# Six raw slots that also hold the low parts, and four slots for the high parts of the split weights

## The chip, the core and the metric

The kernel runs on one core of a Trainium2 chip. A core has TensorE (PE in the profile; PEld is its weight load), VectorE (DVE), ScalarE (ACT), GpSimd (POOL) and SyncE (SP), which here issues nearly all transfers, and 16 DMA engines that bring weights from HBM to SBUF. The engines run programs of their own and wait for each other through semaphores. The metric is device time in microseconds for one execution; the figure given is the median of the runs.

## What is computed

Two blocks of a network for one sequence of 256 positions of width 1024, in float32. The part of the reference that matters here is the products with weights:

```python
def first_block(...):
    h = rms_norm(x, attn_norm_w[i])
    x = x + hybrid_mixer(h, ...)          # w_in (1024 x 7440), SSD and attention, w_ssd_out, w_attn_out, w_out
    h = rms_norm(x, moe_norm_w[i])
    x = x + hier_moe(h, ...)              # 32 experts: gate, up (1024 x 256 each), down (256 x 1024), top 2 of one group
    gate = jax.nn.sigmoid(rms_norm(x, ple_norm_w[i]) @ w_ple_gate[i])
    x = x + gate * (p[i] @ w_ple[i])
    return rms_norm(x, final_norm_w)
```

The second block takes that result: one wide input product, long convolutions by spectra (products with cosine and sine tables), latent attention with 8 heads (products w_uq and w_ukv), gates, and w_hy_out, w_attn_out and w_out.

## The kernel before

**Tiles of dense weights.** Every dense weight is cut into tiles of at most 2048 columns per partition, mostly four chunks of 128 rows by 512 columns (1 MB). There are 80 of them, numbered k in the order in which PE uses them; 42 stand before the experts and 38 behind. To keep float32 accuracy with fast products, each tile is split: SP loads it to a slot of `raw`, ACT copies it rounded to float32r into a slot of `WH` (line 1257), DVE subtracts, `WL = raw - WH` (line 1760), and PE makes three products per chunk, high by high, low by high, high by low (`mul3`, issued at line 519; transposes at line 528).

**Slots and waits.** `raw` has NRAW = 4 slots of 2048 columns, `WH` and `WL` have NSPLIT = 3 each: ten in all. ACT's copy of tile k waits for its load and for PE's use of tile k-3 (semaphore mark `("tile", k-3)`); DVE's subtraction waits for the copy; SP's load of tile k (`fetch`, line 2680) waits for the subtraction of tile k-4, `lo.wait_ge(e, k - NRAW)`.

**Where the splits stand.** ACT and DVE run in order. Calls of `weights(consumed)` stand between their other work; each makes the splits that `Splitting.due` allows, that is of tiles k whose forerunner in the slot is below `consumed`, so up to three ahead. `used(key)` is the number of tiles used when product `key` is done. Typical of ACT is: splits, then the drain of a product from PSUM, then splits. On ACT the drains and other steps are lines 1285 (`drain`), 1289 (`drain_t`), 1295 (sigmoid), 1416 (exponentials), 1671 and 1673 (drains of the key and value product `kv`). On DVE they are line 1800 (`drain_t`), 1867 (convolution), 2072 and 2089 (first block), 2396 (final norm of the first block), 2491 and 2492 (drain of `kv`), 2551 to 2567 and 2583, 2587 (products of the spectra and their results). Each PSUM bank is taken by a new product only when its last reader has drained it (`Ring.take`).

The stretch around `kv` on ACT and DVE is:

```python
            conv_T(1)
            for i in range(2):
                weights(used(("wuq", i)))
                drain_t((("kq", i), 1), KQ[:, 1, 384 * i:384 * i + 384])
            conv_T(2)
            for i in range(2):
                weights(used(("wukv", i)))
                mm.wait_ge(e, (("kv", i), 1))
```

**The experts.** 97 tiles of 1 MB (gate, up and down of 32 experts and `w_ple`) are loaded unsplit by `fetch_held` (line 2710) into 22 buffers. Twelve are parts of arrays that lie free by then, and ten are the slots of the dense tiles: the four raw slots and the six of `WH` and `WL`. The buffers have numbers; 9 to 12 were the raw ones, 13 to 18 the others. Which tile goes to which number is a fixed list, `buffer_of`, and a buffer is loaded again when PE has used its last tile (`held_last`). `held_raw` and `held_split` tell which numbers the dense slots have. Three early groups of expert loads (numbers 0 to 6) stand between the last dense fetches on SP. Behind the experts `weights(None, n)` makes the splits up to tile n at fixed places.

## Time and profile before

| what | value |
|---|---|
| time, median of 3 runs | 813.51 us (813.35 to 814.79) |
| profiled execution, its own time | 810.26 us |
| its span, from the first to the last instruction | 808.4 us |
| mean granted clock of TensorE | 0.973 |
| PE busy | 738.0 us |
| DVE busy | 466.5 us |
| ACT busy | 323.2 us |
| bytes read from HBM | 188.17 MB |

The profiled execution is one of its kind, and shorter than the median of the runs by 3.25 us. Busy time is the time in which an engine had an instruction running; PE's matmuls overlap, so that PE can be shown busy while it doesn't run at its full pace. In a group's row stand its count, busy time and mean of one in ns, then the engine's idle time in front of it and what ended most of that. The idle time in front of an instruction is put down to whatever released it last. The chain that ended last is followed back from the last instruction, step by step, to what released it, or to the instruction in front of it on the same engine.

### The profile page before, as it was taken

What the parts mean: (1) busy time and instruction counts of PE and PEld (TensorE: products, weight loads), DVE (VectorE), ACT (ScalarE), POOL (GpSimd) and SP (SyncE); (2) the same over time, 40 slices, a digit from 0 to 9 for tenths busy, and PEclk for the clock granted to TensorE, in tenths of its full rate; (3) what the DMA queues carried; (4) which work ended last, traced back from release to release, by engine and by line L of the source; (5) the groups of instructions that cost most, each with busy time, mean ns of one, the idle gap of its engine ahead of it and who ended that gap; (6) DMA issues with size and microseconds to landing.
All of it is one profiled execution on the core that took longest, in us unless ns stands there. A gap on an engine that the chain in (4) does not pass through costs nothing.

```text
span 808.4 us, 11003 instructions
## 1 busy us (share of the span) xinstructions
PE 738.0 (91%) x4608; PEld 557.3 (69%) x4608; DVE 466.5 (58%) x825; ACT 323.2 (40%) x479; POOL 17.8 (2%) x14
## 2 busy tenths in 40 slices
PE   4999999999999999996799797689999989799998
PEld 4978886878877886563445354247999856578886
DVE  5779965445866565531243131138677798855673
ACT  5554446536437334210110010036755524255631
POOL 0000000000000000000000000001100003000000
PEclk9999999999999999998789899999999999999999
DMA  9665543233438859799999999996462654333311
GB/s 318 186 213 195 188 141 125 81 105 104 124 112 326 326 223 424 316 372 419 420 420 419 421 422 422 418 388 222 134 233 89 229 186 153 108 105 105 104 53 53
DMA packets 62578, 189.98 MB, mean 235 GB/s; under 512 B 7417, under 2 KB 11771, under 8 KB 50044
## 3 DMA queue, kind: packets, MB, share of 16 engines
q1 hardware_dynamic: 60750, 184.44, 61.2%
q10 hardware_dynamic: 1774, 4.79, 1.7%
q8 instruction: 38, 0.62, 0.3%
q14 instruction: 16, 0.13, 0.1%
HBM read 188.17 MB, written 1.05 MB: 234 GB/s over the span
## 4 chain that ended last, share of the span: by engine, by line
PE 60%; DMA 16%; DVE 14%; ACT 8%; issue 2%; POOL 0%; SPq 0%; ACTq 0%; DVEq 0%
PE pb L519 56%; DMA raw<-in_w_exp_up 8%; DVE WL L1760 4%; PE pb L528 3%; ACT WH L1257 3%; DMA WHo<-in_w_exp_up 3%; DMA WLo<-in_w_exp_up 3%; DMA WLo<-in_w_exp_down 2%; ACT arena L1416 1%; DMA raw<-in_w_in 1%; DVE cv_ L1867 1%; DVE arena L2026 1%; ACT arena L1285 1%; POOL small L2658 0%; DVE arena L1813 0%
## 5 line engine op out<-in xcount | busy, mean ns | idle before, releaser
L1760 DVE TENSOR_TENSOR WL<-raw,WH 128x2048 fp32r<-128x2048 f32 (+5 forms) x80 | 173.4, 2178 | 87.3 <-ACT WH L1257 87.3
L1257 ACT ACTIVATE WH<-raw 128x2048 fp32r<-128x2048 f32 (+5 forms) x80 | 144.9, 1822 | 80.7 <-PE pb L519 71.2
L519 PE MATMUL pb<-WH,HTh 128*128 128x512 f32 (+2 forms) x384 | 156.1, 406 | 6.0 <-ACT arena L1285 3.1
L519 PE MATMUL pb<-WL,HTh 128*128 128x512 f32 (+2 forms) x384 | 148.5, 387 | 0.0
L519 PE MATMUL pb<-WH,HTl 128*128 128x512 f32 (+2 forms) x384 | 148.4, 386 | 0.0
L519 PEld LDWEIGHTS pb<-WH,HTh 128*128 128x128 f32 x384 | 72.8, 190 | 24.8 <-issue 5.1
L519 PEld LDWEIGHTS pb<-WL,HTh 128*128 128x128 f32 x384 | 72.7, 189 | 14.5
L519 PEld LDWEIGHTS pb<-WH,HTl 128*128 128x128 f32 x384 | 73.1, 190 | 13.2 <-issue 1.0
L519 PE MATMUL pb<-WH,arenao 128*128 128x512 f32 x192 | 59.6, 391 | 1.2 <-DVE arenao L1794 1.2
L519 PE MATMUL pb<-arena 128*32 128x256 f32 (+6 forms) x252 | 56.6, 422 | 3.4 <-ACT arena L1673 2.6
L2310 DVE TENSOR_TENSOR rt_<-rt_,pb 128x256 f32<-128x256 f32 x8 | 3.4, 421 | 90.2 <-ACT rt_ L1536 90.2
L519 PE MATMUL pb<-HTh,WH 128*128 128x256 f32 (+1 forms) x184 | 52.5, 285 | 0.2
L519 PE MATMUL pb<-HTh,WL 128*128 128x256 f32 (+1 forms) x184 | 52.0, 283 | 0.0
L519 PE MATMUL pb<-HTl,WH 128*128 128x256 f32 (+1 forms) x184 | 51.9, 282 | 0.0
L519 PE MATMUL pb<-arena,rt_ 128*32 128x512 f32 (+1 forms) x208 | 43.0, 462 | 0.7 <-DVE rt_ L2318 0.5
L1536 ACT ACTIVATE rt_<-pb 128x256 f32<-128x256 f32 x8 | 3.1, 383 | 100.0 <-PE pb L519 100.0
L519 PEld LDWEIGHTS pb<-arena 128*32 128x32 f32 (+4 forms) x252 | 27.1, 159 | 22.4 <-issue 8.8
L519 PEld LDWEIGHTS pb<-WH,arenao 128*128 128x128 f32 x192 | 35.7, 188 | 8.6 <-DVE WL L1760 1.4
L519 PE MATMUL pb<-WHo,arena 128*32 128x256 f32 (+1 forms) x96 | 30.7, 533 | 8.7 <-issue 4.4
L519 PE MATMUL pb<-WL,arenao 128*128 128x512 f32 x96 | 37.4, 390 | 0.0
L519 PEld LDWEIGHTS pb<-HTh,WH 128*128 128x128 f32 (+1 forms) x184 | 34.5, 188 | 0.9 <-DVE WL L1760 0.5
L519 PEld LDWEIGHTS pb<-HTh,WL 128*128 128x128 f32 (+1 forms) x184 | 34.6, 188 | 0.2
(366 smaller groups left out, 1267.7 us busy)
## 6 DMA issues: line engine op xcount, KB each, us to landing
raw<-in_w_in SPq DMA_DIRECT2D x46, 1024.0 KB, 5.2
raw<-in_w_exp_up SPq DMA_DIRECT2D x18, 1024.0 KB, 22.1
arena<-in_w_exp_down SPq DMA_DIRECT2D x14, 1024.0 KB, 13.1
arena<-in_w_exp_gate SPq DMA_DIRECT2D x13, 1024.0 KB, 21.0
raw<-in_w_out SPq DMA_DIRECT2D x8, 1024.0 KB, 5.2
WHo<-in_w_exp_down SPq DMA_DIRECT2D x8, 1024.0 KB, 19.0
WLo<-in_w_exp_down SPq DMA_DIRECT2D x8, 1024.0 KB, 22.2
raw<-in_w_exp_gate SPq DMA_DIRECT2D x7, 1024.0 KB, 13.8
```

The source lines that it names most:

```text
L519: return e.matmul(o, l, r, start=start, stop=stop, skip_group_check=True)
L528: return e.transpose(o, i, ident[0:k, 0:k])
L1257: e.activation(h_, r_, ACT.Copy).then_inc(hi.sem, hi.mark(k))
L1285: e.activation(dst[:, t, :], pb((name, t))[:, 0:n], f, scale=scale).then_inc(ac.sem, ac.mark((name, t)))
L1416: ins = e.activation(S1[s][:, cut], S1[s][:, cut], ACT.Exp, bias=nmx[:, s, t:t + 1], scale=-1.0, accum_out=ssum[:, t, h:h + 1])
L1536: e.activation(HG[q % 2], pb(("gu", q))[:, 0:256], ACT.Silu).then_inc(ac.sem, ac.mark(("su", q)))
L1760: e.tensor_tensor(l_, r_, h_.bitcast(F32), ALU.subtract).then_inc(lo.sem, lo.mark(k))
L1867: e.scalar_tensor_tensor(out=cv[:, s:L], in0=u[:, 0:L - s], scalar=cw[:, 3 - s, g:g + 1], in1=cv[:, s:L], op0=ALU.mult, op1=ALU.add).then_inc(
L2026: ins = e.scalar_tensor_tensor(out=LM[:, h, :], in0=pb(("lm", t, h0))[:, (h - h0) * 128:(h - h0) * 128 + 128], scalar=Ac[:, t, h:h + 1], i ...
L2310: e.tensor_tensor(HG[q % 2], HG[q % 2], pb(("gu", q))[:, 256:512], ALU.mult).then_inc(ve.sem, ve.mark(("gu", q)))
```

## The change

`WL` goes away. The low part is written over the raw weight, in the slot of `raw` (DVE reads `raw` and `WH` and writes `raw`, seen as float32r through `raw_r`). The ten slots are dealt out anew: NRAW = 6 and NSPLIT = 4. A raw slot is now free when PE has used the tile, not when the subtraction is made, so `fetch(k)` waits for `("tile", k - 6)`; ACT's copy waits for `("tile", k - 4)`. `due` gets a fixed distance, AHEAD = 3, which is what NSPLIT was, so that the splits stay at their places in the programs of ACT and DVE. The expert buffers 9 to 18 are named again in the order in which the slots come free: the raw slot of each of the last six dense tiles, and the high slot of each of the last four. All ten now wait for PE's use of a dense tile; the four raw ones had waited for a subtraction. SP's first loads are still issued as four, then two, though the two no longer wait for a slot; behind the experts six dense loads, not four, stand in front of two constants (lines 2762 and 2763).

```diff
--- before.py
+++ after.py
@@ -18,8 +18,9 @@
 L = 256
 D = 1024
 EPS = 1e-6
-NRAW = 4
-NSPLIT = 3
+NRAW = 6
+NSPLIT = 4
+AHEAD = 3
 SLOT = 2048
 SCRATCH = 1024
 CAP = 32
@@ -183,16 +184,15 @@
                    d_wr, d_late, d_filt, d_fw, d_hyb, d_bg, d_bg2, d_fb, d_out]
 
 
-        shared = (("WH", [128, NSPLIT, SLOT], F32R), ("WL", [128, NSPLIT, SLOT], F32R), ("HDh", [128, 1280], F32R),
+        shared = (("WH", [128, NSPLIT, SLOT], F32R), ("raw", [128, NRAW, SLOT], F32), ("HDh", [128, 1280], F32R),
                   ("HDl", [128, 1280], F32R), ("arena", [128, 18944], F32), ("cv_", [128, 1024], F32),
                   ("sg_", [128, 1024], F32), ("XN", [128, 2, D], F32), ("HTh", [128, 8, L], F32R), ("HTl", [128, 8, L], F32R))
         with ExitStack() as other:
-            WHf, WLf, HDhf, HDlf, arena_r, cv_r, sg_r, XN_r, *HTf = (
+            WHf, raw_r, HDhf, HDlf, arena_r, cv_r, sg_r, XN_r, *HTf = (
                 other.enter_context(nc.sbuf_tensor(n + "o", shape, F32 if dt is F32R else F32R))
                 for n, shape, dt in shared)
-        WH, WL, HDh, HDl, arena, cv_, sg_, XN, *HT = (sb(n, shape, dt) for n, shape, dt in shared)
+        WH, raw, HDh, HDl, arena, cv_, sg_, XN, *HT = (sb(n, shape, dt) for n, shape, dt in shared)
         HD_, HDf = (HDh, HDl), (HDhf, HDlf)
-        raw = sb("raw", [128, NRAW, SLOT])
         rt_ = sb("rt_", [128, 2048])
         PV = cv_[:, 512:1024]
         X = sb("X", [128, 2, D])
@@ -399,14 +399,15 @@
             for i in range(2):
                 weight((key, i), w, 8, 512 * i, 512, rows_)
         dense_again = len(tiles)
-        emptied = [(dense_again + i) % NSPLIT for i in range(NSPLIT)]
-        last_raw = [raws[(dense_again + i) % NRAW] for i in range(NRAW)]
+        emptied_raw = [(dense_again - NRAW + i, raws[(dense_again + i) % NRAW]) for i in range(NRAW)]
+        emptied_high = [(dense_again - NSPLIT + i, WHf[:, (dense_again + i) % NSPLIT, :]) for i in range(NSPLIT)]
+        emptied = [x for k in range(dense_again - NRAW, dense_again) for x in [*emptied_raw, *emptied_high] if x[0] == k]
         part = lambda o: arena[:, o:o + 2048]
         held = [part(16896), part(12800), rt_[:, :], part(4096), XN.rearrange("p t d -> p (t d)"), part(10752), part(6144),
-                part(14848), part(8704), *last_raw, *[x[:, s, :] for s in emptied for x in (WHf, WLf)], part(0), part(2048),
+                part(14848), part(8704), *[x for _, x in emptied], part(0), part(2048),
                 part(15168)]
         KF = [held[17], held[18]]
-        held_raw, held_split = (9, 10, 11, 12), 13
+        held_raw, held_high = (9, 10, 11, 13, 15, 17), (12, 14, 16, 18)
         FGU = [held[i].rearrange("p (c n) -> p c n", c=8) for i in (13, 14)]
         FD = held[15].rearrange("p (c n) -> p c n", c=2)
         held_to = {0: 0, 1: 0, 2: 0, 5: 0, 6: 0, 7: 0, 17: 44, 18: 44, 8: 56, 3: 68, 4: 76}
@@ -457,12 +458,13 @@
 
         def tile_parts(k):
             c, n = tiles[k]["shape"]
-            return tuple(x[:, tiles[k]["slot"], 0:c * n].rearrange("p (c n) -> p c n", c=c) for x in (WH, WL))
+            return tuple(x[:, 0:c * n].rearrange("p (c n) -> p c n", c=c)
+                         for x in (WH[:, tiles[k]["slot"], :], raw_r[:, k % NRAW, :]))
 
         def tile_flat(k):
             c, n = tiles[k]["shape"]
             s = tiles[k]["slot"]
-            return WH[:, s, 0:c * n], WL[:, s, 0:c * n], raws[k % NRAW][:, 0:c * n]
+            return WH[:, s, 0:c * n], raw_r[:, k % NRAW, 0:c * n], raws[k % NRAW][:, 0:c * n]
 
         def used(key):
             return chunk_at[key][-1][0] + 1
@@ -479,8 +481,8 @@
 
             def due(self, consumed):
                 while self.k < self.end:
-                    before = tiles[self.k]["before"]
-                    if before is not None and before >= consumed:
+                    first = 0 if self.k < dense_again else dense_again
+                    if self.k - AHEAD >= max(first, consumed):
                         return
                     self.k += 1
                     yield self.k - 1
@@ -1252,8 +1254,7 @@
                     if tiles[k]["before"] is not None:
                         mm.wait_ge(e, ("tile", tiles[k]["before"]))
                     elif k >= dense_again:
-                        i = held_split + 2 * emptied.index(tiles[k]["slot"])
-                        mm.wait_ge(e, held_last[i][0:2], held_last[i + 1][0:2])
+                        mm.wait_ge(e, held_last[held_high[k - dense_again]][0:2])
                     e.activation(h_, r_, ACT.Copy).then_inc(hi.sem, hi.mark(k))
 
             def norm_rows(n, src, after=None):
@@ -1577,7 +1578,7 @@
             weights(None, dense_again + 2)
             ss = norm_of["np"]
             e.activation(XN[:, 0, :], X[:, 0, :], ACT.Square, accum_out=ss[:, 0:1]).then_inc(ac.sem, ac.mark(("sq", "np")))
-            weights(dense_again)
+            weights(None, dense_again + 3)
             po.wait_ge(e, ("rs", "np"))
             weights(used(("wpg", 0)) - 1)
             junk = [rt_[:, 0:512], rt_[:, 512:1024]]
@@ -2369,7 +2370,7 @@
             low("np", NT, 8, pnw)
             weights(None, dense_again + 2)
             norm_sum("np", X)
-            weights(dense_again)
+            weights(None, dense_again + 3)
             weights(used(("wpg", 0)) - 1)
 
             def gated(i, t):
@@ -2672,7 +2673,7 @@
                 if dense_again <= k < dense_again + NRAW:
                     mm.wait_ge(e, held_last[held_raw[k - dense_again]][0:2])
                 elif k >= NRAW:
-                    lo.wait_ge(e, k - NRAW)
+                    mm.wait_ge(e, ("tile", k - NRAW))
                 c, n = tiles[k]["shape"]
                 dst = raws[k % NRAW][:, 0:c * n].rearrange("p (c n) -> p c n", c=c)
                 d = d_w[k % NRAW]
@@ -2700,10 +2701,8 @@
                     mm.wait_ge(e, ("mT", "T", 6))
                 elif i == 8:
                     ve.wait_ge(e, ("mg", 1))
-                elif i in held_raw:
-                    lo.wait_ge(e, dense_again - NRAW + held_raw.index(i))
-                elif i < held_split + 6:
-                    mm.wait_ge(e, ("tile", dense_again - NSPLIT + (i - held_split) // 2))
+                elif i < 19:
+                    mm.wait_ge(e, ("tile", emptied[i - 9][0]))
                 else:
                     mm.wait_ge(e, (("wo", 1), 1))
                 w = wpl if name[0] == "wpl" else dict(gate=wg, up=wu, down=wd)[name[0]][4 * name[1] + name[2]]
@@ -2713,7 +2712,7 @@
             xr = A["x"].rearrange("a (t p) d -> p (a t) d", p=128)
             for t in range(2):
                 e.dma_start(X[:, t, :], xr[:, t, :]).then_inc(d_x.sem, d_x.mark("in", by=16))
-            for k in range(NRAW):
+            for k in range(4):
                 fetch(k)
             for dst, src in ((rows[0:40, :], A["conv_w"].rearrange("a k (j p) -> (a k j) p", p=128)),
                              (rows[40:50, :], A["conv_b"].rearrange("a (j p) -> (a j) p", p=128)),
@@ -2730,7 +2729,7 @@
             turned_part = lambda a: a.rearrange("a n -> (a n)")[64:96].partition_broadcast(128)
             for dst, n in ((dtb, "dt_bias"), (alog, "a_log"), (dsk, "d_skip")):
                 e.dma_start(dst, bc(A[n])).then_inc(d_early.sem, d_early.mark("in", by=16))
-            for k in range(NRAW, 6):
+            for k in range(4, 6):
                 fetch(k)
             for dst, src in ((mnw, pc(A["moe_norm_w"], 8)), 
                              (snw, pc(A["ssd_norm_w"], 8)), (rb[:, 0:4], bc(A["b_router_group"])),
```

## Rows read from the trace of the kernel before

**Rows 1.** The page: busy shares, chain by engine, costliest groups with idle time before.

```profile
PE 738.0 (91%) x4608; PEld 557.3 (69%) x4608; DVE 466.5 (58%) x825; ACT 323.2 (40%) x479; POOL 17.8 (2%) x14
...
PE 60%; DMA 16%; DVE 14%; ACT 8%; issue 2%; POOL 0%; SPq 0%; ACTq 0%; DVEq 0%
...
L1760 DVE TENSOR_TENSOR WL<-raw,WH 128x2048 fp32r<-128x2048 f32 (+5 forms) x80 | 173.4, 2178 | 87.3 <-ACT WH L1257 87.3
L1257 ACT ACTIVATE WH<-raw 128x2048 fp32r<-128x2048 f32 (+5 forms) x80 | 144.9, 1822 | 80.7 <-PE pb L519 71.2
```

**Rows 2.** Who waited for whom, whole span: us in total, times, longest.

```profile
PE pb L528 <- DVE arena L2587: 4.3, 1, 4.3
...
PE pb L519 <- ACT arena L1285: 3.1, 4, 2.0
...
PE pb L519 <- ACT arena L1673: 2.6, 1, 2.6
...
PE pb L519 <- DVE WL L1760: 1.1, 1, 1.1
```

**Rows 3.** Busy time by stretch: PE, PEld, DVE, ACT, POOL, clock, DMA share, GB/s.

```profile
362.00:540.00 178.00, 146.30 (x1190) 72.32 (x1182) 43.16 (x101) 19.68 (x36) 0.00 (x0) 0.89 1.01 418
```

**Rows 4.** Timeline of DVE from 654 us: start, us, what, idle before.

```profile
654.37 0.67 DVE L2551 TENSOR_TENSOR XN<-pb,arena 128x512 f32<-128x512 f32 x1
...
655.38 0.69 DVE L2553 TENSOR_TENSOR sg_<-pb,arena 128x512 f32<-128x512 f32 x1 [0.33 <-PE pb L519]
656.10 0.69 DVE L2555 TENSOR_TENSOR XN<-XN,sg_ 128x512 f32<-128x512 f32 x1
```

**Rows 5.** Timeline of ACT from 255 us.

```profile
265.75 1.92 ACT L1257 ACTIVATE WH<-raw 128x2048 fp32r<-128x2048 f32 x1 [3.52 <-PE pb L519]
```

**Rows 6.** Timeline of ACT from 630 us.

```profile
641.26 1.91 ACT L1257 ACTIVATE WH<-raw 128x2048 fp32r<-128x2048 f32 x1 [1.69 <-PE pb L519]
...
645.91 1.92 ACT L1257 ACTIVATE WH<-raw 128x2048 fp32r<-128x2048 f32 x1 [1.87 <-PE pb L519]
...
649.13 1.91 ACT L1257 ACTIVATE WH<-raw 128x2048 fp32r<-128x2048 f32 x1 [0.77 <-PE pb L519]
...
651.21 0.37 ACT L1673 ACTIVATE arena<-pb 128x256 f32<-128x256 f32 x1
```

**Rows 7.** Timeline of DVE from 630 us.

```profile
643.20 2.29 DVE L1760 TENSOR_TENSOR WL<-raw,WH 128x2048 fp32r<-128x2048 f32 x1 [0.47 <-ACT WH L1257]
...
647.86 2.29 DVE L1760 TENSOR_TENSOR WL<-raw,WH 128x2048 fp32r<-128x2048 f32 x1 [1.29 <-ACT WH L1257]
...
651.08 2.29 DVE L1760 TENSOR_TENSOR WL<-raw,WH 128x2048 fp32r<-128x2048 f32 x1 [0.26 <-ACT WH L1257]
```

**Rows 8.** The chain that ended last, from 640 us: start, us, what.

```profile
646.02 3.03 PE pb L519 x12
...
651.64 32.02 PE pb L519 x110
...
683.68 0.70 DVE sg_ L2553
```

**Rows 9.** Timeline of PE from 640 us.

```profile
646.02 0.50 PE L519 MATMUL pb<-WH,HDh 128*128 128x512 f32 x1 [0.21 <-DVE arena L1800]
```

**Rows 10.** Timeline of DVE from 34 us.

```profile
40.05 2.29 DVE L1760 TENSOR_TENSOR WL<-raw,WH 128x2048 fp32r<-128x2048 f32 x1 [0.17 <-ACT WH L1257]
42.26 5.79 DVE L1867 SCALAR_TENSOR_TENSOR cv_<-pb,small,cv_ 128x255 f32<-128x255 f32 x12
```

**Rows 11.** Timeline of SP's queue from 282 us.

```profile
313.24 20.26 SPq L2710 DMA_DIRECT2D arena<-in_w_exp_down  x2
```

**Rows 12.** Loads of dense tiles after 540 us, issue to landing.

```profile
DMA to landing us min/median/max: 2.1/5.0/8.2
```

**Rows 13.** The chain that ended last, from 515 us.

```profile
521.97 13.18 DMA WLo<-in_w_exp_down
```

**Rows 14.** Timeline of DVE from 573 us.

```profile
576.08 2.35 DVE L2396 TENSOR_TENSOR XN<-X,arena 128x1024 f32<-128x1024 f32 x2
```

## The prediction, made before the change was run

> **What bounds the kernel now.** I read the page first (busy shares, chain, costliest groups), then who PE waits for, then ACT and DVE around the places where PE waits. PE is busy for 91% of the span; the chain that ended last lies on PE for 60% of it, on DMA for 16%, on DVE for 14% and on ACT for 8% [rows 1]. Before the ACT half of the split (line 1257) ACT sits idle for 80.7 us in all, and 71.2 us of that end with a PE matmul [rows 1]. This is the wait that the change loosens. But PE's own waits are short: 4.3 us for line 2587, 3.1 us in four pieces for line 1285, 2.6 us for line 1673, 1.1 us for a low part [rows 2]. Between 362 and 540 us the transfers run at 418 GB/s with a DMA share of 1.01 and PE is busy for 146.3 of 178 us: the expert stage is bound by transfers [rows 3], and no split lies in it. So the 71 us are no sum of gains. They count only where the next instruction of ACT or DVE is one that PE waits for.
>
> **The change part by part.** A dense weight tile k is loaded to a raw slot and split by ACT into a high part, then by DVE into a low part. Before, ACT's copy of k waits until PE has used tile k-3, and the load of k until the low part of k-4 is made. After, the copy waits for PE's use of k-4, and the load for PE's use of k-6. The order in every engine's program stays.
>
> *The low part in place.* The 80 subtractions keep number and shape (mean 2178 ns [rows 1]). No row has a split in place, but there are neighbours of like shape: 128x512 written over one of its operands takes 0.69 us (line 2555), written elsewhere 0.67 and 0.69 us (lines 2551, 2553) [rows 4]. So 0 to +0.02 us each; at most some 16 splits lie in the chain (its 14% on DVE hold other work too), 0 to +0.3 us. I take 0, by the pair at 655.38 and 656.10.
>
> *High parts with a fourth slot.* The common freed wait looks as at 265.75 us: ACT idles 3.52 us for PE, copies for 1.92 us, and so on; the two add up to 5.44 us, the time in which PE uses a tile of four 512-wide chunks, and PE waits for none of these copies, which run two tiles ahead [rows 2, 5]. Such a wait is worth 0: what is late next is ACT's own next instruction, which waits for PE again. The skill's page Perfetto Trace Analysis (Identifying Performance Opportunities) says that one gap repeating on the engine that should be saturated can mean too few buffers; here it repeats on ACT, which need not be saturated, so the rule, read for ACT, would promise far more than PE's waits can give.
>
> A freed wait matters where PE needs an ACT or DVE result standing behind the split. The one large place is 641 to 652 us. I number the tiles there: 58 and 59 hold three chunks of 384 columns, 60 and 61 two of 512, 62 to 64 four of 512.
> - ACT copies 62 at 641.26 after 1.69 us idle, until PE has used 59. It will need 58 only and can start when ACT is free, at 639.57. DVE's low part of 62 then doesn't wait the 0.47 us in front of 643.20, and the drain behind it (line 1800) comes 0.47 us earlier. PE waited for it 0.21 us before 646.02. Gain 0.2 us, which ends PE's use of 61 at 648.9 and not 649.1 (3.03 us from 646.02) [rows 6 to 9].
> - ACT copies 63 at 645.91 after 1.87 us idle. It will need 59 only and goes right behind the drains, at about 643 to 645. Then come the drain of 60, when PE has ended it (645.9), and the copy of 64, which will need 60 and not 61: about 646.5 to 648.5. Before, it stood at 649.13 to 651.04, in front of the drain of 61 (lines 1671 and 1673), which ended at 651.58 and for which PE had waited 2.6 us. Now that drain needs only PE's end of 61: 648.9 plus some 0.6 us, 649.5. PE started at 651.64 and will start at 649.55: 2.1 us gained [rows 2, 6, 8].
> - DVE must follow, or PE gives it back. From 643.20 to line 2551 at 654.37 it takes 11.17 us, of which 1.29 and 0.26 us are idle for ACT's copies; without them, and from 642.73 on, it gets there at 652.35, 2.0 us earlier. The product behind it (655.38) had to wait 0.33 us for PE, and PE's side comes 2.1 us earlier [rows 4, 7].
> - From there the chain lies on PE for 32.0 us to 683.68 and then on DVE's products up to PE's wait for line 2587. Both feeders have moved by 2.0 to 2.1 us, so the whole chain has. Freed waits later in it add nothing, since at 683.68 DVE waits for PE [rows 8].
>
> The second place is 38 to 53 us. ACT's copy in front loses its wait for PE, but DVE loses only the 0.17 us in front of its split at 40.05; 5.79 us of unbroken DVE work follow [rows 10], ACT's next copy hangs on their end, and PE waited 1.1 us for the low part after that [rows 2]. Gain 0.2 us, as DVE was the slow one; the upper bound is 1.1. The four waits for line 1285 (3.1 us [rows 2]) are for drains that stand in front of their copy, or behind exponentials that wait for DVE: between 0 and 3.1, and I take 0, as the copies next to them show no idle time for PE.
>
> *Loads that wait for PE's use of k-6.* Old and new event lie within about one tile of use, 5.4 us, of each other, and everything behind a fetch on SP's queue moves with it. Expert tiles stand behind the last dense fetches. Their cover: SP issues the twentieth or so at 313.24 and then stands 20.3 us for a free buffer [rows 11], so 5.4 us of delay reach nobody; without that cover they would be paid in full. At the small tiles the lead is shortest: PE ends 59 at 641.2, and 59 has 18 matmuls of 384 columns where 61 has 12 of 512 in 3.03 us, so 3.4 us, and 58 ends at 637.8. Tile 64 is fetched then; landing takes 5.0 us in the median and 8.2 at most after 540 us [rows 12], which makes 642.8 to 646.0, against 646.5 when ACT wants it. Cost 0, with 0.5 to 3.7 us in hand. If it came later, the drain of 61 behind it on ACT, and PE, would wait.
>
> *Into the expert stage and back.* Expert tiles use as many buffers as before in the same order; a few first fills can go a little earlier or later, and the stream stops for lack of buffers at 313 in either case: 0 [rows 11]. At the other end PE waits for the last expert tile, issued at 521.97 and landed 13.18 us later [rows 13]. The next dense loads follow it, and the fifth and sixth now without waiting for a split. At 418 GB/s [rows 3] a load of 1.05 MB takes 2.5 us, so the fifth goes out from about 533 on, 2 us before that landing; shared evenly among six loads this could cost 0.4 us. 0 to +0.4, taken as 0, since loads of one queue land in a row. The skill's page DMA: Bandwidth & Descriptors (Queues, rings and completion order) has descriptors consumed in ring order, which gives 0 too; no row here tests it. Two constants (lines 2762, 2763) now stand behind the sixth load, which waits for the last expert products, at about 540; line 2396 reads one at 576.08 [rows 14], 36 us later: 0.
>
> **The sum.** 2.1 + 0.2 = 2.3 us off the profiled execution: its span goes from 808.4 to 806.1 us, its own time from 810.26 to 808.0. It lies 3.25 us under the median of the runs, 813.51; I carry that difference over: 811.2 us (-0.28%).
>
> **Rivals.**
> - *PE's gain becomes a longer wait for line 2587.* If DVE's chain from 654 us doesn't move, because its splits of 63 and 64 don't close up (ACT's copies stand behind drains and come later than worked out), PE arrives 2.1 us earlier and waits 6.4 us there, not 4.3. For it: that wait shows DVE as the slower side by then. Against it: the three idle stretches of DVE from 643 to 651 all end with ACT's copy [rows 7]. Time 813.3. The change may also do nothing of what it says: copies that stay where they stood need not use a fourth slot ahead. The time is the same.
> - *The freed waits are worth more.* The 3.1 us of line 1285, or what is left of the 1.1 us at 53, move up: up to 3 us more, 808.2 to 810.2. Against it: no idle time for PE in front of those copies.
> - *Slower: a raw tile comes late*, since its slot is held through PE's use. From PE's end of 58 to the copy of 64 there are 8.7 us; each us over that is paid by ACT's drain and PE. The 2.3 us are gone at 11.0 us of landing, and a loss of 1.7 us, 815.2, stands at 12.7. The longest landing after 540 us was 8.2 [rows 12]; among expert loads 13.2 occur [rows 13].
>
> **How the numbers follow.** Forecast 0.54, absorbed 0.24, more 0.12, slower 0.10. A measurement of this kernel can tell about 0.2%, 1.6 us, from no change. The forecast's own range is 810.2 to 812.2 (splits in place 0.3, the seam 0.4, half a microsecond for medians of runs that spread by 1.4 us); 0.48 of its chance lies below 811.9 and 0.06 above. Faster 0.48 + 0.12 = 0.60; same 0.06 + 0.24 = 0.30; slower 0.10. The range takes in the absorbed case with its spread and part of the larger gain: 809.4 to 813.8.
>
> **What would show it.** PE's wait for line 1673 falls from 2.6 us to about 0.5; DVE's splits from 641 to 652 stand without idle time; the wait for line 2587 stays at 4.3 us (6.4 under the first rival); ACT's idle time for PE before its copies falls well below 71 us while PE's busy time stays; SP's waits turn from DVE to PE, and no copy but the first is released by a raw load; the expert stage keeps its length and rate. The prediction is wrong if PE shows a new wait for a split, or if the products from 654 us on start no earlier.

## The result and the profile after

The changed kernel takes 806.24 us in the median of 19 runs (804.75 to 811.66), the kernel before 812.78 us in as many. One run of the latter, of 1719.87 us, is left out of the ratio, which is 0.9923, with an interval from 0.9907 to 0.9939: 6.3 us less. The forecast was 811.2 us, with a range from 809.4 to 813.8. The direction was right and the size was not: the time lies 5.0 us below the forecast and below the range.

The profiled execution of the changed kernel has an own time of 809.5 us and a span of 807.7 us; it is one of the longer ones of its kind. Lines of the changed kernel stand one or two below those of before: 519 is now 521, 528 is 530, 1257 is 1258, 1760 is 1761, 1285 is 1286, 1289 is 1290, 1673 is 1674, 2587 is 2588, and the low part is called `rawo`. The edits of the experiments move some of them by a few lines more. The page shows busy shares, then groups with count, busy time, mean of one in ns and idle time in front:

```profile
PE 740.9 (92%) x4608; PEld 560.7 (69%) x4608; DVE 465.1 (58%) x825; ACT 322.1 (40%) x479; POOL 17.8 (2%) x14
...
L1761 DVE TENSOR_TENSOR rawo<-raw,WH 128x2048 fp32r<-128x2048 f32 (+5 forms) x80 | 172.7, 2175 | 72.7 <-ACT WH L1258 72.6
...
L1258 ACT ACTIVATE WH<-raw 128x2048 fp32r<-128x2048 f32 (+5 forms) x80 | 143.9, 1821 | 20.8 <-PE pb L521 15.1
```

Beside [rows 1], ACT's idle time in front of its copies has fallen from 80.7 to 20.8 us, and the part that ends with a PE matmul from 71.2 to 15.1 us. The low part written in place takes 2175 ns, as before (2178).

Who PE waits for, in total, times and longest, to hold beside [rows 2]:

```profile
PE pb L530 <- DVE arena L2588: 4.3, 1, 4.3
PE pb L521 <- ACT arena L1286: 3.1, 4, 2.0
...
PE pb L521 <- DVE rawo L1761: 0.9, 1, 0.9
PE pb L521 <- ACT arena L1674: 0.7, 1, 0.7
```

Of these four one has changed by more than 0.3 us, that for `kv`'s drain: 2.6 us before, 0.7 us now. The timeline of ACT around it, to hold beside [rows 6]:

```profile
643.45 1.91 ACT L1258 ACTIVATE WH<-raw 128x2048 fp32r<-128x2048 f32 x1
...
647.21 1.93 ACT L1258 ACTIVATE WH<-raw 128x2048 fp32r<-128x2048 f32 x1
649.39 0.38 ACT L1672 ACTIVATE arena<-pb 128x256 f32<-128x256 f32 x1 [0.25 <-PE pb L521]
649.67 0.38 ACT L1674 ACTIVATE arena<-pb 128x256 f32<-128x256 f32 x1
```

The copies of 63 and 64 have no idle time in front of them, and the last drain waits for nothing but PE. The timeline of DVE, to hold beside [rows 4, 7], shows its splits without idle time as well:

```profile
643.43 2.28 DVE L1761 TENSOR_TENSOR rawo<-raw,WH 128x2048 fp32r<-128x2048 f32 x1
...
646.70 2.28 DVE L1761 TENSOR_TENSOR rawo<-raw,WH 128x2048 fp32r<-128x2048 f32 x1
...
649.57 2.28 DVE L1761 TENSOR_TENSOR rawo<-raw,WH 128x2048 fp32r<-128x2048 f32 x1
...
652.85 0.67 DVE L2552 TENSOR_TENSOR XN<-pb,arena 128x512 f32<-128x512 f32 x1
```

The size of this gain can be read on PE without regard to what came earlier, from the transposes ahead of `kv` to the first product behind it. Before, then after:

```profile
641.00 1.11 PE L528 MATMUL pb<-c,XN 128*128 128x128 f32 x8
...
651.64 3.70 PE L519 MATMUL pb<-arena 128*128 128x512 f32 x8 [2.60 <-ACT arena L1673]
```

```profile
641.81 1.11 PE L530 MATMUL pb<-c,XN 128*128 128x128 f32 x8
...
650.10 5.42 PE L521 MATMUL pb<-arena 128*128 128x512 f32 x12 [0.75 <-ACT arena L1674]
```

That is 10.64 us before and 8.29 us after, 2.35 us gained; the prediction had 2.1. So the place that was forecast behaves as forecast, and most of the extra gain lies elsewhere. The other place that was forecast, PE's wait for a low part at 53 us, has 0.28 us less, where 0.2 were forecast. Before, then after:

```profile
52.97 0.50 PE L519 MATMUL pb<-WH,HTh 128*128 128x512 f32 x1 [1.13 <-DVE WL L1760]
```

```profile
52.46 0.50 PE L521 MATMUL pb<-WH,HTh 128*128 128x512 f32 x1 [0.85 <-DVE rawo L1761]
```

One part of the extra gain shows when the timelines of the front are laid side by side. ACT before, and then PE before:

```profile
91.89 1.91 ACT L1257 ACTIVATE WH<-raw 128x2048 fp32r<-128x2048 f32 x1 [3.53 <-PE pb L519]
93.71 1.06 ACT L1289 ACTIVATE arena<-pb 128x512 f32<-128x512 f32 x2
```

```profile
91.63 2.02 PE L528 MATMUL pb<-c,arena 128*128 128x128 f32 x17
...
94.87 0.47 PE L519 MATMUL pb<-WH,HTh 128*128 128x512 f32 x1 [0.65 <-ACT arena L1289]
```

ACT and PE after:

```profile
91.76 0.60 ACT L1290 ACTIVATE arena<-pb 128x512 f32<-128x512 f32 x1 [3.90 <-PE pb L530]
```

```profile
91.13 2.02 PE L530 MATMUL pb<-c,arena 128*128 128x128 f32 x17
...
93.57 0.48 PE L521 MATMUL pb<-WH,HTh 128*128 128x512 f32 x1
```

Before, a copy that had waited 3.53 us for PE stood in front of the drains of line 1289. They stood at 93.71 and stand at 91.76 now, and PE had waited 0.65 us for one of them. PE's transposes start 0.5 us earlier after the change, the product behind them 1.3 us earlier: PE is 0.5 us ahead by 91 us, and 0.8 us more behind this place. Of the 0.5 us, 0.28 are the wait at 53 us. The rest stands ahead of 24 us, where two profiled executions of one kernel differ as much: the 96 matmuls that start at 69.81 us before start at 69.30 in the first profile of the changed kernel and at 69.80 in its third. So the front gives 1.1 us in the traces. The second profiled execution of the changed kernel has an own time of 806.5 us and was slowed by the clock (below) in the same places as that of before; it lies 3.8 us under 810.26, and 1.3 and 2.35 make 3.65 of them.

The rest is as it was. In the expert stage (busy time by stretch, as in [rows 3]) PE's busy time, the clock and the rate have hardly moved:

```profile
362.00:540.00 178.00, 146.56 (x1188) 73.99 (x1181) 43.17 (x100) 18.91 (x35) 0.00 (x0) 0.88 1.01 418
```

### The profile page after: what moved, and what is told of

It reads as the page before. It is cut to its first block, busy times and chain, and to the rows that moved or that the text cites. A ratio compares the mean times of both kernels' runs of the same rounds, so it can differ in the third digit from the quotient of the medians.

```text
span 807.7 us, 10974 instructions
## 1 busy us (share of the span) xinstructions
PE 740.9 (92%) x4608; PEld 560.7 (69%) x4608; DVE 465.1 (58%) x825; ACT 322.1 (40%) x479; POOL 17.8 (2%) x14
## 4 chain that ended last, share of the span: by engine, by line
PE 60%; DVE 16%; DMA 13%; ACT 7%; issue 2%; POOL 0%; SPq 0%; ACTq 0%; DVEq 0%
PE pb L521 57%; DMA raw<-in_w_exp_up 6%; DVE rawo L1761 5%; DMA WHo<-in_w_exp_up 4%; PE pb L530 4%; ACT WH L1258 3%; DMA WHo<-in_w_exp_down 2%; DVE cv_ L1868 1%; ACT arena L1417 1%; DMA raw<-in_w_in 1%; DVE arena L2027 1%; DVE arena L1814 1%; ACT arena L1286 1%; POOL small L2659 0%; DVE arena L2073 0%
## 5 line engine op out<-in xcount | busy, mean ns | idle before, releaser
L1761 DVE TENSOR_TENSOR rawo<-raw,WH 128x2048 fp32r<-128x2048 f32 (+5 forms) x80 | 172.7, 2175 | 72.7 <-ACT WH L1258 72.6
L1258 ACT ACTIVATE WH<-raw 128x2048 fp32r<-128x2048 f32 (+5 forms) x80 | 143.9, 1821 | 20.8 <-PE pb L521 15.1
L521 PE MATMUL pb<-rawo,HTh 128*128 128x512 f32 (+2 forms) x384 | 148.8, 388 | 0.0
L521 PEld LDWEIGHTS pb<-rawo,HTh 128*128 128x128 f32 x384 | 73.1, 190 | 14.7
L521 PE MATMUL pb<-arena 128*32 128x256 f32 (+6 forms) x252 | 58.5, 433 | 1.6 <-ACT arena L1674 0.7
L521 PE MATMUL pb<-raw,arena 128*32 128x256 f32 (+1 forms) x256 | 48.9, 474 | 10.6 <-DMA raw<-in_w_exp_up 5.9
L521 PE MATMUL pb<-HTh,rawo 128*128 128x256 f32 (+1 forms) x184 | 52.0, 282 | 0.0
L521 PE MATMUL pb<-WHo,arena 128*32 128x256 f32 (+1 forms) x160 | 42.6, 491 | 9.7 <-DMA WHo<-in_w_exp_up 9.4
L521 PE MATMUL pb<-rawo,arenao 128*128 128x512 f32 x96 | 37.4, 390 | 0.0
L521 PEld LDWEIGHTS pb<-raw,arena 128*32 128x32 f32 (+1 forms) x256 | 19.9, 136 | 23.5 <-issue 10.8
```

The costliest lines, as they stand in the source:

```text
L521: return e.matmul(o, l, r, start=start, stop=stop, skip_group_check=True)
L1258: e.activation(h_, r_, ACT.Copy).then_inc(hi.sem, hi.mark(k))
L1761: e.tensor_tensor(l_, r_, h_.bitcast(F32), ALU.subtract).then_inc(lo.sem, lo.mark(k))
```

## The experiments

Each kernel was timed in five rounds beside the kernel before; all ratios are to that, with 95% intervals. First the two kernels of the comparison, unedited, to have more than one profiled execution of each.

**The changed kernel again.**

> The changed kernel once more, unedited, for a second profile at a granted clock near that of the kernel before (0.973; the first profile of the changed kernel had 0.966). Theory A (the gain lies in dense stages: 0.2 to 1.2 us in front of 139 us, 2 us at 651 us, and the rest, some 3 us, is TensorE's clock in the expert stage, which differs from execution to execution): time ratio to before 0.992 to 0.994, and stages other than 320 to 540 us no more than 4 us shorter than before. Theory B (the expert stage itself is shorter, from its buffers' new order or places): 320 to 540 us is 3 us or more shorter at the same granted clock. Theory C (nothing but a bias between profiles): ratio 0.997.

806.64 us, ratio 0.9936 [0.9914, 0.9958]. The ratio is the one of theory A, but its reason isn't borne out: from the matmul that starts at 331.2 us before to the one at 537.4 it takes 206.2 us before, and 206.6 and 205.8 us in the two profiles of the changed kernel. That refutes theory B and leaves no 3 us for the expert stage. The first profile, 3.0 us longer than this one, has a fall of the granted clock at 232.9 us that this one lacks, and a fall at 704 us twice as long.

**The kernel before again.**

> The kernel before once more, unedited. Ratio 1.000 within 0.002. Its second profile tells what a usual execution looks like: if the first one (810.26 us) was a fast one, this one stands at 812 to 814 us, and the 2 to 4 us more lie at one place. Theory A: in 362 to 540 us with a lower clock. Theory B: in 362 to 540 us at the same clock, with longer waits for transfers.

813.16 us, ratio 1.0014 [0.9999, 1.0029]. The second profile (813.43 us) is 3.2 us longer than the first, as expected, but neither theory has the place: by 362 us 0.4 us of it are there and at 540 us 0.6, then 1.7 come behind the wait at 650 us and 1.0 behind the one for line 2587 (the clock, below).

**The old wait alone.** ACT's copies wait for the tile three before again, and everything else of the change stays.

```diff
                     elif k >= dense_again:
                         mm.wait_ge(e, held_last[held_high[k - dense_again]][0:2])
+                    if k - AHEAD >= (0 if k < dense_again else dense_again):
+                        mm.wait_ge(e, ("tile", k - AHEAD))
                     e.activation(h_, r_, ACT.Copy).then_inc(hi.sem, hi.mark(k))
```

> The changed kernel, but ACT's copy of tile k waits for PE's use of k-3 as before (four slots, of which one is never used ahead). My forecast's mechanism (the freed waits): PE's wait for line 1674 comes back to 2.6 us and the ratio loses its 2.3 to 3.3 us, so 0.996 if the measured 0.9923 holds other gains too. If all of the gain were the freed waits: 1.000. If the freed waits were worth only what the first profile shows: 0.995 to 0.997. If the gain is of the loads and slots alone: 0.992.

812.52 us, ratio 1.0003 [0.999, 1.0015]. The whole gain goes, and PE's wait for `kv`'s drain is back at 2.60 us. The low part in place, six raw slots, loads that wait for PE's use of k-6 and the new order of the expert buffers are worth nothing together that this can see, which leaves the copies' wait.

**The old wait behind the experts only** (`if k - AHEAD >= dense_again:`).

> As the one before, but the wait for k-3 is kept only behind the experts; in front of them the fourth slot is used. Tells the part of the freed waits in front (1.2 us by the first profile of the changed kernel at 139 us, part of it lost again by 253 us) from the part behind (2.0 us at 651 us). Forecast: 2.0 us slower than the changed kernel and 0 to 1.2 us faster than the one with the wait everywhere.

810.35 us, ratio 0.9979 [0.9966, 0.9992]. Some 1.7 us of the gain belong to the front (0.7 to 2.8 by the interval) and the larger part to what stands behind the experts: 3.7 us, where 2.0 were expected.

**The old wait at three copies behind the experts.**

```diff
-                    if k - AHEAD >= (0 if k < dense_again else dense_again):
+                    if k in (62, 63, 64):
```

> The changed kernel, but ACT's copies of tiles 62, 63 and 64 alone wait for PE's use of the tile three before, as all did before the change. Theory A (one place behind the experts: the drain of kv behind the copy of 64, and what PE's long wait does to the granted clock): PE's wait for line 1674 is back at 2.6 us, and the time is that of the kernel with the wait at all tiles behind the experts (810.35), so 810.0 to 810.7, 3.5 to 4 us over the changed kernel (806.64). Theory B (the gain behind the experts is spread over many copies): the place itself is worth the 2.1 us of the prediction and no more, so 808.7, and the remaining 1.6 us stay with the other copies.

811.32 us, ratio 0.9991 [0.9969, 1.0014]. Three copies take back what all copies behind the experts do: there is one place, and it is worth more than the 2.35 us of its wait. Some five microseconds separate this kernel from the changed one (4.5 to 5.5 by the ratios). Theory B's 808.7 lies outside the interval (ratio 0.995).

**The old wait at four copies of the front** (`if k in (15, 16, 17, 18):`).

> The changed kernel, but ACT's copies of tiles 15, 16, 17 and 18 alone wait for PE's use of the tile three before. Theory A (the gain in front of the experts has a second place at 91 to 106 us, where such a copy stood in front of the drain of line 1289): 0.7 us of the front gain go, 807.3, and ACT's drain at 91.8 us of the span stands 1.9 us later again. Theory B (the front gain lies at 38 to 53 us alone, as forecast): no change, 806.6.

808.22 us, ratio 0.9948 [0.9928, 0.9967]. That is 1.6 us over the changed kernel (806.64), by ratios 1.0 to 2.0 us over its three measurements, though their intervals overlap. In the trace the copy stands at 92.33 us in front of the drains again, now at 94.15. PE, from the 96 matmuls ahead to the product behind the drains:

```profile
70.25 22.00 PE pb L521 x96
...
95.31 0.47 PE L521 MATMUL pb<-WH,HTh 128*128 128x512 f32 x1 [0.65 <-ACT arena L1292]
```

That is 25.06 us, as before (from 69.81 to 94.87), where the changed kernel takes 24.27 (from 69.30 to 93.57). So the front's second place exists and is worth 0.8 us, most of the 1.1 us that the traces give the front.

### The clock behind PE's long waits

Why is the place at 650 us worth more than its wait? The chain that ended last gives the stretch behind it as one piece of 102 matmuls (start, us, what). The kernel with the old wait everywhere, then the changed one:

```profile
651.97 28.31 PE pb L521 x102
```

```profile
650.10 28.29 PE pb L521 x102
```

The kernel before in its second profile, and the one with the old wait at three copies:

```profile
652.20 29.97 PE pb L519 x102
```

```profile
649.35 29.98 PE pb L521 x102
```

The same matmuls take 1.67 us longer in the last two. The stretches there (us, busy time of PE, PEld, DVE, ACT and POOL, clock, DMA share, GB/s), second profile of before and three old waits:

```profile
653.60:657.00 3.40, 3.40 (x6) 1.34 (x5) 2.00 (x7) 1.48 (x1) 0.00 (x0) 0.50 1.01 331
```

```profile
649.80:653.20 3.40, 3.40 (x5) 1.35 (x4) 2.84 (x7) 1.03 (x1) 0.00 (x0) 0.51 0.42 164
```

For 3.4 us the granted clock is 0.50, that is 1.2 GHz and not 2.4, and PE works at half its pace: 1.7 us are lost, which is what the chain shows. Ahead of it PE had stood for 2.6 us. Of six profiles with this wait at its 2.6 us, two (before in its first profile, and the old wait everywhere) show no such fall, and four do: before in its second, and those with the old wait behind the experts, at three copies, and (below) before with one copy moved. Of nine profiles in which the wait is 0.7 us none has a fall there. The prediction rested on one execution that happened to have none.

The Trainium skill, in TensorE: Matmul & The Clock Gate (What's actually happening), has the clock follow how busy PE has been, and its note there has the number of slow matmuls at a kernel's start vary between runs of one kernel. The traces agree with the first, with 0.50 behind the wait in four of six profiles; what they show to vary lies in the middle of the kernel.

A second such wait is that for line 2588, 4.3 us, unchanged by the change. In each of the eleven profiles that have it at 4.2 or 4.3 us with nothing laid into it, the clock falls right behind it. Two tests followed: fill a wait with matmuls that nobody reads, which leaves its end where it was, or shorten it by other means.

**Idle matmuls in the wait at 650 us.** The old wait everywhere, and

```diff
+            def warm(n, name, by, m):
+                by.wait_ge(e, name)
+                for _ in range(n):
+                    mul(pb(name)[:, :], m[:, 0:128], m[:, 0:512])
+
...
                 gemm(("kv", i), ("wukv", i), CKT, "ckT", (ve, ac))
+            warm(5, ("u", 2, 0), ve, C["fc"])
```

> The changed kernel with the wait for tile three before at all copies (812.52 before), and five matmuls of 128x512 that nobody reads in PE's program behind kv, where PE stands idle for 2.6 us: about 0.43 us each, 2.2 us in all, inside the wait. They leave the wait's end where it is. Theory A (the wait costs more than its length, since in part of the executions the granted clock falls to 0.5 right behind it): the fall at 650 to 657 us does not show in the profile, and the median falls by what the falls cost on average, 0.5 to 1.7 us, to 810.8 to 812.0. Theory B (the falls come by themselves and have nothing to do with the wait): the time stays at 812.5 or rises by up to 0.3.

813.15 us, ratio 1.0002 [0.9981, 1.0024]. Badly sized: a plain float32 matmul of 512 columns shows as two records of 0.43 us, so five of them took 4.2 us. From the start of `kv`'s last twelve matmuls to the first product with a low part behind it, it takes 13.6 us, and 12.2 without the idle ones: 1.4 us were added. The ratio is that of the same kernel without them (1.0003) all the same; that leans to theory A. With three:

> As the kernel with the wait for tile three before at all copies and idle matmuls behind kv, but three of them, not five: the trace showed 0.86 us for each and not 0.43, so five overran the wait of 2.6 us by 1.7 us and three fill it just. Theory A (the wait costs more than its length through the granted clock): 810.8 to 812.0. Theory B: 812.5, with up to 0.3 more.

812.01 us, ratio 0.9988 [0.9972, 1.0004]. No fall at 650 us in either profile, three of them fit the wait (12.2 us again), and a ratio 0.0015 lower than without them, 1.2 us, with intervals that overlap. It leans the same way and doesn't settle it.

**Idle matmuls in the wait for line 2588.** The changed kernel, and in front of the wait

```diff
+            warm(9, ("uf", 1, 1, "fc"), ve, C["fc"])
             ve.wait_ge(e, ("ui", 1, 0), ("ui", 1, 1))
             transposed("uT", lambda t: U[:, t, 2, :], 4, turned=True)
```

> The changed kernel as it is, and nine matmuls of 128x512 that nobody reads in PE's program in front of its wait for line 2588 (4.3 us): 3.9 us in all, inside the wait. Theory A (the wait makes the clock fall right behind it, to 0.5 for 3.4 or 6.8 us at 704 to 711 us, in every profile so far): the fall goes and with it 1.5 to 3 us, 803.6 to 805.1. Theory B (the fall is not tied to PE's wait): 806.6 or up to 0.3 more, and the fall stays.

807.62 us, ratio 0.9928 [0.9903, 0.9952]. The nine took 7.7 us, 3.4 us more than the wait, and still the ratio is that of the changed kernel, and the time 1.0 to 1.4 us over it: something gave back most of what the overrun cost. The profile has no fall at 704 us. With five:

> As the changed kernel with idle matmuls in front of PE's wait for line 2588, but five of them, not nine: nine took 7.7 us and overran the wait of 4.3 us by 3.4 us, and still the time was that of the changed kernel. Theory A (the fall of the clock hangs on the wait and costs 2 to 3 us): 803.8 to 805.0, no fall in the profile at 704 us. Theory B: 806.6.

804.43 us, ratio 0.9898 [0.9877, 0.9919]: 2.2 us less than the changed kernel, and nothing was done but to keep PE running while it waited. The intervals overlap at their ends (the changed kernel's first is [0.9907, 0.9939]), but five of the six runs lie at or below 804.76 us, and only two of the changed kernel's 31. The place in the changed kernel (second profile), from the transposes behind the wait to the next ones, and the clock:

```profile
703.30 1.88 PE L530 MATMUL pb<-c,arena 128*128 128x128 f32 x8 [4.26 <-DVE arena L2588]
...
708.69 0.60 PE L530 MATMUL pb<-c,arena 128*96 128x128 f32 x4
```

```profile
703.60:707.00 3.40, 3.40 (x13) 3.01 (x13) 3.05 (x3) 1.19 (x2) 0.00 (x0) 0.50 0.00 0
```

The same with five idle matmuls (the ten records at 698.33):

```profile
698.33 4.45 PE L521 MATMUL pb<-arena 128*128 128x512 f32 x10
702.75 1.23 PE L530 MATMUL pb<-c,arena 128*128 128x128 f32 x8
706.58 0.60 PE L530 MATMUL pb<-c,arena 128*96 128x128 f32 x4
```

```profile
702.00:710.00 8.00, 6.89 (x34) 5.04 (x33) 5.50 (x6) 3.49 (x5) 0.00 (x0) 1.00 0.21 62
```

From transposes to transposes it takes 5.39 us at the fallen clock and 3.83 us at the full one. In the changed kernel's first profile the fall is twice as long, and the same stretch takes 6.12 us (705.52 to 711.64). So a fall costs 1.6 to 2.3 us here, and here it is shown to come with the wait: the wait's end is where it was (PE goes on 0.05 us behind DVE's product in both, which ends at 703.25 and 702.69 us), PE's idleness is gone, and the fall with it, in both kernels with idle matmuls here against eleven of eleven profiles without.

### Versions that beat both kernels

What makes the wait for line 2588 long? DVE, in the changed kernel's profile, stands idle in front of one split:

```profile
692.03 1.40 DVE L1814 SCALAR_TENSOR_TENSOR arena<-pb,small,arena 128x512 f32<-128x512 f32 x2
695.93 2.29 DVE L1761 TENSOR_TENSOR rawo<-raw,WH 128x2048 fp32r<-128x2048 f32 x1 [2.50 <-ACT WH L1258]
```

ACT's copy of tile 68 stands behind the two sigmoids of gate 0, which wait for this same drain of DVE, though ACT had been idle for long. It is moved:

```diff
                 elif name[0] == "gate" and i < 2:
+                    if i == 0:
+                        weights(None, 69)
                     sigmoid(i)
```

> The changed kernel, and ACT's copy of tile 68 placed in front of the two sigmoids of gate 0 instead of behind them (its slot is free, since it needs PE's use of 64). DVE then doesn't stand 2.5 us for it at 691 us. Theory A (behind the experts PE and DVE bind in turn, and what stands in front of line 2588 on DVE sets PE's wait of 4.3 us): the wait falls to 1.8 us and the time to 804.1. Theory B (something else that arrives at the same time sets that wait): it stays at 4.3 us and the time at 806.6.

801.74 us, ratio 0.9853 [0.984, 0.9866]: 5 us below the changed kernel, 11 below the kernel before. DVE, and PE behind it:

```profile
693.68 1.40 DVE L1816 SCALAR_TENSOR_TENSOR arena<-pb,small,arena 128x512 f32<-128x512 f32 x2
695.00 2.28 DVE L1763 TENSOR_TENSOR rawo<-raw,WH 128x2048 fp32r<-128x2048 f32 x1
```

```profile
704.59 1.23 PE L530 MATMUL pb<-c,arena 128*128 128x128 f32 x8 [1.67 <-DVE arena L2590]
...
708.42 0.60 PE L530 MATMUL pb<-c,arena 128*96 128x128 f32 x4
```

The wait is down from 4.3 to 1.7 us, and behind it the stretch takes 3.83 us, the one of the full clock: 2.6 us from the wait and 1.6 us from the clock, 4.2 of the 5 us.

The profiled execution took 806.30 us, the longest of the six, and one reason lies in the front, where nothing was moved: the clock is at 0.50 for 6.8 us there (columns as in the stretches above), and PE loses 3.2 us.

```profile
232.80:239.60 6.80, 6.80 (x15) 4.38 (x14) 4.67 (x5) 0.00 (x0) 0.00 (x0) 0.50 0.24 93
```

A fall stands at this place in four of the seventeen profiles (this one, the changed kernel's first and those of two more), and PE's wait ahead of it is 0.78 us there as in the profiles without. So a long wait is not the only thing behind which the clock falls.

**The split of 68 later on DVE as well**, behind the products of lines 2584 and 2588:

```diff
                 else:
+                    end, splitting.end = splitting.end, 68
                     fill(4)
...
                         e.tensor_tensor(uv, uv, ZH[:, t, :], ALU.mult).then_inc(ve.sem, ve.mark(("ui", o_, t)))
+                        splitting.end = end
```

> As the kernel with the copy of 68 in front of the sigmoids, and DVE's split of 68 (2.29 us) moved behind the products of lines 2584 and 2588. Theory A: DVE reaches line 2588 another 2.3 us earlier, PE's wait is gone, time 802.3; if the fall of the granted clock at 704 us hangs on that wait, it goes too, and the time is 800 to 801.5. Theory B: 806.6, or more, as the drains behind the split come 2.3 us later.

802.48 us, ratio 0.9865 [0.9845, 0.9884]. The wait for line 2588 is gone, but one of 2.3 us appears a little later, for the drain of line 1816 that stands behind the split now, and the clock falls behind that one (0.50 from 710.4 us). Nothing is gained over the first move. Theory A's 802.3 us is met by luck, since neither theory had this wait.

**The move without the change.** The changed kernel a third time, and beside it the kernel before with the one moved copy.

> The changed kernel, unedited, beside the two others of this call on one chip. 806.2 to 806.7, ratio 0.992 to 0.994 to the kernel before.

806.85 us, ratio 0.9925 [0.9906, 0.9945].

> The kernel before, with nothing of the change, and ACT's copy of tile 68 in front of the two sigmoids of gate 0. It needs PE's use of 65 then, which ends well before the sigmoids, so the copy is as early as in the changed kernel. Theory A (DVE's idle 2.5 us in front of its split of 68, and the fall of the clock behind PE's wait, are worth 4 to 5 us in any version): 808 to 809.5. Theory B (the move pays only with four slots): 812.7.

807.74 us, ratio 0.9948 [0.9927, 0.9968]. The old kernel with one copy moved is within 1 us of the changed one. PE's wait for that product is 1.7 us here too, with no fall behind it. That gain needs no fourth slot, and theory B falls.

**Idle matmuls in the front wait too.** The changed kernel with the moved copy, and two idle matmuls in PE's wait of 2.0 us at 165 us (`if j == 8: warm(2)`, into the bank that is taken next).

> The changed kernel with the copy of 68 in front of the sigmoids (801.74), and two idle matmuls of 0.86 us in PE's wait of 2.0 us at 165 us, ahead of the first chunk that waits for ACT's drain of z. Theory A (a long wait of PE makes the clock fall behind it): the fall at 168 us is gone in the profile, and the time is 1 to 1.5 us less, 800.3 to 800.8. Theory B (the fall comes by itself): 801.7 and up to 0.3 more.

801.32 us, ratio 0.986 [0.9837, 0.9883]. The clock there, in the changed kernel's second profile and in this one:

```profile
167.70:171.10 3.40, 3.40 (x13) 2.82 (x12) 2.72 (x2) 1.14 (x2) 0.00 (x0) 0.50 0.01 3
```

```profile
165.00:172.00 7.00, 6.75 (x37) 5.07 (x36) 2.76 (x2) 3.74 (x7) 0.00 (x0) 1.00 0.35 136
```

The fall is absent in the one profile, but five of the sixteen profiles with the wait as it was have none there either, and the time is that of the moved copy alone, 0.4 us less where theory A had 1 to 1.5. Whether the fall hangs on this wait is open. It costs 1.6 us where it stands, and it stands in all six profiles with the old wait throughout the front, and in five of the ten others.

## Why the prediction was wrong

**The diagnosis held.** PE's short waits, not ACT's 71 us, bounded the gain; the wait for line 1673 fell from 2.6 to 0.7 us (0.5 forecast), and DVE followed. The term of 2.1 us measured 2.35. The wait for line 2587 stayed at 4.3 us, as forecast, so the rival in which it takes the gain is refuted. The low part in place, six raw slots, later loads and the seam at the experts were put at 0, and the old wait alone brings the whole time back (1.0003), so together they are 0 within 0.15%. No raw tile came late: a load released ACT's copy once, at the first tile. The loads of SP's queue landed in the order of their issue in both traces, all 179, as the zero for the seam took it.

**The step that failed first: the front taken as one place ("Gain 0.2 us"), and "between 0 and 3.1, and I take 0" for the drains beside the copies.** I looked for places in the list of PE's waits, and took the long ones. The first place gave 0.28 us, as forecast. The second place of the front shows in that list as 0.65 us for line 1289, far down, and is worth 0.8 us. It stood plainly in the chain of waits and on ACT's timeline: a copy with idle time for PE in front of it and a drain right behind it, at 91.89. The rule of the prediction ("a freed wait matters where PE needs an ACT or DVE result standing behind the split") was right; it was applied to two places when every copy had to be walked through. So the front gives 1.1 us in the traces, where 0.2 were forecast. In the runs it is 1.7 us, from 0.7 to 2.8.

**The step that failed most: a wait of PE was priced at its length.** Behind the 2.6 us at 649 us the granted clock falls in four of six profiles, for 1.67 us each, 1.1 us on average, and behind the 0.7 us of the changed kernel in none of nine. That this wait makes it fall is likely and not shown; the test that shows it was made at line 2588. The profiled execution of before had none, so no row of that stretch showed it; but it had one at 708 us behind the wait of 4.3 us, and the clock was never set beside PE's waits.

**The base.** The difference of 3.25 us between the profiled execution and the median was carried over; the median of 19 runs of before is 812.78, which puts the base 0.7 us too high.

The miss of 5.0 us is thus 0.7 for the base, 0.25 at `kv`, 0.9 in the front, and 1.1 for the clock: some 3.0 us. Not settled are the remaining 2 us. The timed runs put the place at 650 us at four to five microseconds, where its profiles say 2.35 without a fall and 4.0 with one; falls may be more frequent in the timed executions than four in six, and further falls, as that at 708 us lasting 6.8 us in before's second profile and 3.4 in its first, may come more often in a kernel that stands more. The one at 168 us, 1.6 us each, is in all six profiles with the old wait in the whole front and in five of the nine with the new one; the one at 232 us is in none of those six and in four of those nine, and works the other way. The timed runs give only a mean clock for each, so this was argued and not shown.

**The rival "the freed waits are worth more"** had the right sign and named the drains, but of line 1285, whose waits didn't move (3.1 us before and after), and its range ended at 808.2.

## What to carry to other kernels

List every instruction of a feeder that waits for the bottleneck engine and has a drain right behind it in program order, and walk through all of them; the list of the bottleneck's own waits hides the short ones. Price a wait of PE at its length plus what the granted clock loses behind it, and look into more than one profiled execution before a stretch is called free of it, or before two kernels are compared by one profile each: two profiles of one kernel lay 3 us apart, mostly through such falls, and that is half of what the change gives. When such a wait can't be shortened, matmuls that nobody reads are worth a try, no longer than the wait; but first look whether one copy placed ahead of an instruction that waits anyway makes it shorter: here that gave 4 to 5 us, the whole change 6.

## What was not expected of the hardware

The granted clock fell to 0.50 behind PE waits of 4.2 to 4.3 us in eleven of eleven profiles, behind the wait of 2.6 us in four of six, and behind the one of 1.7 us (the moved copy) in none of three. It fell behind one of 0.78 us at 232 us too, in four of seventeen, so the length of the wait alone doesn't tell. A fall of 3.4 us cost 1.6 to 1.7 us of time. Idle matmuls in a wait kept the clock at 1.00 and took 2.2 us off the kernel. Plain float32 matmuls of 128x512 took 0.86 us each in two records (nine in 7.7 us), where one on float32r operands takes 0.25 us (twelve in 3.03 us [rows 8]).
